# Feed-forward part of a decoder step: a loop of four passes on five engines, and the same work written out

## What is computed

```python
def residual_update(x, conv_o, pool_o, nsa_o, w_out, g2, w_gu, w_down):
    x = x + jnp.concatenate([conv_o, pool_o, nsa_o], axis=-1) @ w_out
    gu = rmsnorm(x, g2) @ w_gu
    return x + (jax.nn.silu(gu[..., :D_FF]) * gu[..., D_FF:]) @ w_down
```

## Time and profile before

| | us |
|---|---|
| median of 3 runs | 1573.87 |
| lowest and highest of them | 1573.78, 1579.42 |
| the profiled execution, its own time | 1573.92 |
| its span, first to last instruction | 1572.1 |
| from gu(2) to gu(10) in it | 574.73 |

### The profile page before, as it was taken

One profiled execution on the slowest core, in us unless ns is written; L12 is line 12 of the kernel. 1 busy time (PEld: TensorE's weight loads), 2 busy tenths in 40 slices (PEclk: granted clock), 3 DMA queues, 4 the chain that ended last, 5 costly groups with the idle time before them and its releaser, 6 DMA issues.

```text
span 1572.1 us, 22952 instructions
## 1 busy us (share of the span) xinstructions
PE 1481.1 (94%) x8743; PEld 1346.4 (86%) x8743; DVE 769.4 (49%) x1538; ACT 473.6 (30%) x950; POOL 263.8 (17%) x326
## 2 busy tenths in 40 slices
PE   6999999987999999899999999999999999999993
PEld 6999987656667666799999999999999999999992
DVE  5499942017988775322425242434344343425364
ACT  5112125035666666423212112111111111112112
POOL 2114104014322200144210101010000001010005
PEclk9999999999999999999999999999999999999996
DMA  8721206620000001233111120202020211202012
GB/s 207 187 62 29 64 8 185 192 69 1 1 1 1 1 1 41 55 83 82 54 34 48 38 71 12 71 16 69 16 67 25 60 44 39 74 11 71 17 38 111
DMA packets 148766, 88.63 MB, mean 56 GB/s; under 512 B 34466, under 2 KB 145017, under 8 KB 148577
## 3 DMA queue, kind: packets, MB, share of 16 engines
q1 hardware_dynamic: 146161, 78.22, 17.8%
q0 software_dynamic: 2496, 8.88, 2.1%
HBM read 78.33 MB, written 13.19 MB: 58 GB/s over the span
## 4 chain that ended last, share of the span: by engine, by line
PE 84%; DVE 6%; issue 3%; ACT 3%; POOL 1%; DMA 1%; SPq 1%; ACTq 0%; DVEq 0%; POOLq 0%
PE psC L1005 16%; PE psB L1005 16%; PE psA L1005 15%; PE psD L977 6%; PE psA L725 4%; PE psC L674 4%; PE psB L725 4%; PE psC L725 3%; PE psD L674 2%; PE psA L1034 2%; PE psC L1034 2%; PE psB L1034 2%; PE psA L855 1%; DVE ybuf L1559 1%; POOL accf L2096 1%
## 5 line engine op out<-in xcount | busy, mean ns | idle before, releaser
L2087 POOL TENSOR_TENSOR hid<-hid,rstdB 128x352 f32<-128x352 f32 x66 | 74.7, 1162 | 653.9 <-ACT hid L1404 653.9
L1345 ACT CAST wH<-wraw 128x1024 fp32r<-128x1024 f32 (+1 forms) x140 | 89.5, 643 | 213.4 <-PE psC L1005 93.3
L977 PE MATMUL psD<-probTb,kvtok 128*128 128x512 f32 x264 | 135.0, 594 | 3.2 <-ACT featT L1337 3.1
L1786 DVE TENSOR_TENSOR wL<-wraw,wH 128x1024 fp32r<-128x1024 f32 (+1 forms) x140 | 111.9, 800 | 42.6 <-ACT wH L1345 42.6
L1005 PE MATMUL psA<-gH,wH 128*128 128x352 f32 x352 | 114.4, 325 | 0.6 <-DVE wL L1786 0.6
L1005 PE MATMUL psB<-gH,wH 128*128 128x352 f32 x352 | 113.7, 323 | 0.0
L1005 PE MATMUL psC<-gH,wH 128*128 128x352 f32 x352 | 113.5, 323 | 0.0
L1005 PE MATMUL psA<-gH,wL 128*128 128x352 f32 x352 | 113.0, 321 | 0.0
L1005 PE MATMUL psA<-gL,wH 128*128 128x352 f32 x352 | 112.9, 321 | 0.0
L1005 PE MATMUL psC<-gL,wH 128*128 128x352 f32 x352 | 112.9, 321 | 0.0
L1005 PE MATMUL psB<-gH,wL 128*128 128x352 f32 x352 | 112.8, 321 | 0.0
(11 more groups left out here) (408 smaller groups left out, 4011.7 us busy)
## 6 DMA issues: line engine op xcount, KB each, us to landing
wraw<-in_w_gu SPq DMA_DIRECT2D x44, 512.0 KB
wraw<-in_w_down SPq DMA_DIRECT2D x88, 128.0 KB
zraw<-in_w_in SPq DMA_DIRECT2D x12, 512.0 KB
xa<-in_x_prompt SPq DMA_DIRECT2D x8, 512.0 KB, 8.3
pages<-in_cache_cmp_kv SPq DMA_DIRECT2D x32, 128.0 KB, 2.4
xs<-in_x_prompt SPq DMA_DIRECT2D x8, 512.0 KB, 3.7
out_y_prompt<-xo SPq DMA_DIRECT2D x8, 512.0 KB, 4.9
out_new_win_sample<-in_cache_win_kv POOLq DMA_DIRECT2D x1, 4064.0 KB, 22.8
```

The lines of the kernel that those rows point to most:

```text
L977: mm = pe.matmul(o, kvtok[:, kt, vc:vc + P], pt, start=first, stop=((g, br) == ORDER[-1] and x == len(g_tiles(n)) - 1))
L1345: sc_.copy(wH[:, par, 0:nk, :], wraw[:, par, 0:nk, :]).then_inc(s["wH_done"], 1)
L1786: dve.tensor_tensor(wL[:, par, 0:nk, :], wraw[:, par, 0:nk, :], wH[:, par, 0:nk, :].bitcast(F32), ALU.subtract).then_inc(s["wL_done"], 1)
L2087: pool.tensor_tensor(hid[:, n, :], hid[:, n, :], rstdB[:, c0:c0 + cw], ALU.mult).then_inc(s["up_scaled"], 1)
```

## The change

The loop is gone from `ffn_order`. A Python loop writes the nine pairs dn(f), gu(f + 2) one after the other for all five engines, with f and w as constants. The order of jobs, the work in each and all waits keep their sense. Lines move up by 1 (ahead of `ffn_order`) or 6 (behind it).

```diff
-        def ffn_order(eng, gu, dn):
+        def ffn_order(gu, dn):
             gu(0, WB)
             gu(1, WB + WGU)
-            at = WB + 2 * WGU
-            with eng.Fori(0, NLOOP) as t:
-                for x in range(2):
-                    w = t * (2 * (WGU + WDN)) + (at + (WGU + WDN) * x)
-                    dn(t * 2 + x, w)
-                    gu(t * 2 + (x + 2), w + WDN)
-            f = 2 * NLOOP
-            at += f * (WGU + WDN)
-            dn(f, at)
-            gu(f + 2, at + WDN)
-            dn(f + 1, at + WDN + WGU)
-            dn(f + 2, at + 2 * WDN + WGU)
+            w = WB + 2 * WGU
+            for f in range(NF - 2):
+                dn(f, w)
+                gu(f + 2, w + WDN)
+                w += WDN + WGU
+            dn(NF - 2, w)
+            dn(NF - 1, w + WDN)
...
-            ffn_order(sp, load_gu, load_dn)
+            ffn_order(load_gu, load_dn)
...
-            ffn_order(pe, gu, dn)
+            ffn_order(gu, dn)
```

More of the change, by code:

```diff
@@ L54 @@
 NF = KF // FT
-NLOOP = (NF - 3) // 2
 WB = KD
@@ L1419, in _ @@
             gu_par = [0]
-            ffn_order(sc_, gu, dn)
+            ffn_order(gu, dn)
             base = 3 * KD * (NF - 1) + 1
@@ L1886, in _ @@
             gu_par = [0]
-            ffn_order(dve, gu, dn)
+            ffn_order(gu, dn)
             scale_back(KD - 2)
@@ L2088, in gu @@
                                            ).then_inc(s["up_scaled"], 1)
-            ffn_order(pool, gu, lambda f, w: None)
+            ffn_order(gu, lambda f, w: None)
             pool.wait_ge(s["unit_mm"], WB + NF * WGU + (NF - 2) * WDN)
```

## The result

The changed kernel takes 1556.47 us (median of 4 runs, 1555.25 to 1557.59). The kernel before took 1574.59 beside it (4 runs, 1573.78 to 1579.42). The ratio is 0.9878, 95% interval 0.9856 to 0.9901: 1.2% faster.

The account below looks back on a forecast made before the run. PE, busy 94% of the span, was taken to bound the kernel. Three branches save 14.48 us, less 0.6 for a late load: 13.9 off 1573.92 gives 1560.0 us, range 1557.5 to 1566.0.

Parts of the forecast that it names:

- What bounds it, and where: Feed-forward part: PE busy 94% of the span, so time is saved only where PE stops, between passes.
- PE's stops at three places: At dn(2) and two later pass boundaries: removing PE's taken branches back saves 4.48, 5.52 and 4.48, together 14.48 us.
- The wait taken off, 0.76 us: PE's wait inside a pass for the weights of m = 1, absent at branches, returning three times; already subtracted from 14.48.
- The reading of the gaps: At each branch PE fetches the target's piece, gets three matmuls, waits for the next piece, then runs at a lower clock.
- Register instructions go on all five engines: Feed-forward loop: 85 register instructions a pass on PE hide beside matmuls, so removing them was costed at nothing.
- The bound of 0.9 us: Most that register instructions on ACT and DVE could cost at PE's 0.76 us wait: a tenth of a microsecond, nine places.
- One more delayed load, 0.6 us: Later gu: sliding instruction fetches delay one more w_gu load, costing 0.6 us; bounds -0.8 to 6.6 us.
- the low end: Whole kernel: lower limit of the forecast range, 1557.5 us, allowing 0.8 for no late weights and 0.9 for registers.
- Waits for weights in place of the gaps: Rival, chance 0.11: w_gu loads come late at most of the eight later gu, leaving about 1565 us.
- Gaps that stay: Rival, chance 0.05: the branch is cheap and gaps belong to starting a dn, so time stays 1573.6 to 1574 us.
- The clock: Rival, chance 0.03: PE running some 850 us without rest is granted the lower clock; 60 us of it gives 1585.

## Why PE fetched its loop anew in each pass

The body has 1813 instructions on PE. "Runtime: NRT & Kernel Launch" in the Trainium skill, section on instruction fetch mechanics, gives blocks of 16 KiB, 256 instructions each, and 2048 instructions of room for PE. By that the body fits, in 7.1 blocks. The same section of the Trainium skill also says that a taken branch whose target is not among the two current blocks stalls for a fetch; by that it would not be held. The trace of before has the stall: in 956 to 1398 us its queue fetched 30 pieces. Three kernels ask why. The first only adds a hint at the head of each pass that names the branch and its target; the second leaves out work to make the body shorter; the third has a body that can't fit.

```diff
-            with eng.Fori(0, NLOOP) as t:
+            with nc.Fori(0, NLOOP, engines=[eng.engine], hint_back_edge=True) as t:
```

> The loop of before, with a hint instruction at the head of each pass, on every engine, that names the branch and its target. Theory (the gaps are PE fetching the code that a taken branch leads to): the first gap of each place goes, since the target is fetched ahead, and the second may stay, for the next piece is asked for only then: 4 to 14 us less than before, 1560 to 1570. Rival (the gaps are the start of a dn or the branch's own handling): the hint changes nothing, 1574 within 1 us.

Measured: 1560.26 us, ratio 0.9919 (0.9897 to 0.9941). Windows of this kernel, gu(3) to gu(4) and gu(4) to gu(5), and all its DMA queues between 956 and 1398 us:

```profile
933.88:1004.01 70.13, 69.21 (x433) 68.70 (x433) 27.68 (x54) 12.56 (x24) 6.73 (x6) 1.00 0.16 45
1004.01:1074.01 70.00, 69.24 (x433) 68.72 (x433) 27.58 (x54) 12.49 (x24) 6.73 (x6) 1.00 0.15 45
```
```profile
## 3 DMA queue, kind: packets, MB, share of 16 engines
q1 hardware_dynamic: 38560, 19.14, 14.9%
issues: line engine op xcount, KB each, median us to landing
```

The row q8 is missing: not one instruction is fetched in three passes, both gaps are gone, and a branch back costs 0.13 us. The theory was too small. The hint does not bring the target earlier here: with it PE no longer loses the target.

The next kernel has no hint. It leaves out one of the three products in the gu of the loop, so 192 matmuls in a gu instead of 288, 672 in the body instead of 864.

```diff
-                    for wt, mv in ((wH, mH), (wH, mL), (wL, mH)):
+                    for wt, mv in ((wH, mH), (wH, mL), (wL, mH))[0:3 if low else 2]:
...
-                    unit(w + x, x % 2, KD, gH, gL, free)
+                    unit(w + x, x % 2, KD, gH, gL, free, low=isinstance(f, int))
```

> The loop of before, no hint, head where it was; PE leaves out the product of the weights' low part with the data in the eight gu of the loop, so its body has 672 matmuls, 1429 instructions (5.6 pieces of 16 KB) instead of 1813 (7.1), and a pair takes about 54 us. Theory (PE keeps about eight pieces; the piece behind the loop's end, fetched ahead of the branch, throws out the piece with the head, and each piece after it likewise): with room to spare nothing is thrown out: instruction fetches stop after the first pass until the last, and no issue gap over 0.3 us stands at the three places. Rival (a branch back always fetches its target, whatever the body's size): two fetches and two issue gaps of 1.3 to 2 us stay at each.

Its windows, gu(3) to gu(4) across the branch, and gu(4) to gu(5); its queues from 936 to 1288 us; and PE's waits from 865 to 1320:

```profile
918.51:973.53 55.02, 54.19 (x337) 53.68 (x337) 27.68 (x54) 12.56 (x24) 6.72 (x6) 1.00 0.20 58
973.53:1028.70 55.17, 54.29 (x337) 53.71 (x337) 27.70 (x55) 12.53 (x24) 6.72 (x6) 1.00 0.20 57
```
```profile
## 3 DMA queue, kind: packets, MB, share of 16 engines
q1 hardware_dynamic: 39104, 19.40, 19.0%
issues: line engine op xcount, KB each, median us to landing
```
```profile
PE psB L1005 <- DVE wL L1787: 6.0, 8, 0.8
PE psA L1005 <- DVE wL L1787: 0.2, 1, 0.2
```

No fetch and no issue gap, with the same loop and the same head. (Its time of 1439.67 us is that of less work.) So a body of 5.6 pieces stays on the chip and one of 7.1 does not, unless hinted. The two blocks of the Trainium skill are too few for both runs. How much PE keeps can be narrowed by counting. Thirty fetches in three passes are ten a pass. With its head ten instructions before the end of a piece, the body of before lies in nine pieces, and PE fetches the one behind it as well. With the head at the start of a piece it lies in eight, and there the queue has three transfers fewer over the span than the 79 of rows 8, so nine a pass:

```profile
q8 instruction: 76, 1.25, 0.3%
```

The body of 1429 lies in seven and, with the one behind, makes eight, which are kept. This fits the Trainium skill's 2048 instructions, eight blocks, if the piece behind the end takes the place of the oldest, which holds the head, and so on round the loop. But the hinted body lies in nine if its head is where it was, and its fetches up to 955 us come at the same points as in the kernel before. None of the nine is fetched again, and eight places do not hold nine. No record shows which piece is thrown out, so how PE keeps the hinted body stays open.

The last pair has two passes of four pairs, so one branch back and a body that is twice as long, without and with the hint (the diff is `Fori(0, 2)` with `range(4)` and factors of 4 for 2).

> Two passes of four pairs, so one taken branch back, between gu(5) and gu(6), head where it was, registers in all eight pairs. Theory (4.5 to 5.5 us a branch, 0.30 us a pair for registers): gu(5) to gu(6) 74 to 76 us, the seven others 70.0, gu(2) to gu(10) 564.5 to 565.5; some 9 us less than before, 1564 to 1565. Rival (the cost grows with the size of the body): the one place takes 10 us or more.

> As the kernel with two passes, with the hint at the head of each. The body is 3500 instructions and more, which PE can't have kept, so here the hint must bring the head's piece ahead of the branch. Theory (the hint steers the fetch): instruction fetches every 20 us all through both passes, but the place between gu(5) and gu(6) takes 70.1 to 70.5 us, or some 72.5 if only the first gap goes and the second stays, since the head lies near the end of its piece. Rival (the hint only helped because all of the body stayed on the chip): the place takes 74 to 76 us as without it.

Measured: 1564.13 us (ratio 0.9936, 0.9914 to 0.9958) and 1559.73 (0.9919, 0.9891 to 0.9946). The window from gu(5) to gu(6) of the first, then that of the second with its queue of instructions in 956 to 1398 us:

```profile
1076.06:1150.40 74.34, 71.06 (x434) 70.26 (x433) 28.55 (x54) 12.79 (x24) 5.71 (x6) 0.98 0.15 44
```
```profile
1073.43:1143.57 70.14, 69.22 (x434) 68.70 (x433) 27.67 (x54) 12.57 (x24) 6.73 (x6) 1.00 0.16 46
...
q8 instruction: 23, 0.38, 0.4%
```

One branch costs 4.3 us with a body of twice the length, so the price is one of the place, not of the size. With the hint it is 0.14 us although PE fetches all the time. So the hint does both: PE keeps this body of 1813 instructions with it, and has the target ahead of the branch where the body is too long to keep.

## Fetches and the gate weights

A fetch that starts while SP's load of gate weights runs was seen to delay gu(2) before, and in the changed kernel gu(7). The next kernel moves PE's code. It was meant to move it by 40 instructions.

```diff
             for m in range(KD):
                 out_unit(m)
+            for _ in range(20):
+                pe.matmul(bank[7][:, 0:8], ident, ident[:, 0:8], start=True, stop=True)
```

> The changed kernel, with 20 matmuls of 8 columns more on PE ahead of the feed-forward part: its code moves by 40 instructions, so PE fetches about 3.2 us earlier against the pairs. The fetch hit gu(7) when it began 7.0 us ahead, and did nothing from 12.7 to 9.8 or from 3.7 us ahead on. Theory (a fetch that starts in the load of the gate weights delays them): no wait for wL at gu(7), and waits of 0.2 to 0.6 us at gu(2) and gu(9), whose fetches move to 6.9 and 6.2 us ahead. Rival (the hit is chance from run to run): it stays at gu(7), or goes anywhere. The time within 1 us of the changed kernel, 2 us for the added matmuls aside.

PE's waits in this kernel, 865 to 1440 us, and the added matmuls in its timeline:

```profile
PE psB L999 <- DVE wL L1782: 5.4, 8, 0.7
```
```profile
743.77 5.17 PE L1036 MATMUL psD<-cpk 128*128 128x8 f32 x40
```

The wait at gu(7) went, as expected; those expected at gu(2) and gu(9) did not come. The twenty matmuls written stand in the trace as forty matmuls and forty weight loads, so the code moved by 80 instructions, and the fetches by some 6 us in place of 3.2. That ahead of gu(2) started 9.6 us before it, that ahead of gu(4) 6.75 us before it and did next to nothing (0.07 us).

The 14 profiles of this case together say more. Take the moment at which a gu would have started, its start less PE's idle time just ahead of it. A fetch 5.3 to 5.7 us ahead of that moment came with such an idle time each time, eight of eight, 0.56 to 1.09 us. One 6.6 to 6.9 us ahead did so twice in nine, with 0.25 at gu(7) of the changed kernel and 0.09 at gu(7) of the version further down. Other idle times at the start of a gu were 0.35 (fetch 2.7 us ahead), 0.12 (11.6 ahead), 0.07, and 0.16 in the kernel with the short body, where no fetch was near, so a load can be a little late without one.

Between 3.6 and 5.3 us and between 5.7 and 6.6 us ahead no profile has a fetch. So the hit depends on the moment, as was thought, and the time in which a fetch costs over half a microsecond is at most 3 us long, not the 4 to 5 us of the load. The kernels without the loop on PE had one such idle time or none in nine gu.

The kernel also took 1564.01 us (ratio 0.9943, 0.9925 to 0.9961), 7.5 more than the changed one. The added matmuls took 5.1 us in place of the 2 allowed for: they start 0.11 us apart, and 0.21 from 747.5 on, where the clock fell. Its windows, 745 to 749, then gu(0):

```profile
745.00:749.00 4.00, 4.00 (x31) 4.00 (x31) 2.09 (x2) 1.99 (x2) 1.36 (x2) 0.81 0.04 8
749.00:755.00 6.00, 6.00 (x23) 6.00 (x24) 0.00 (x0) 0.00 (x0) 0.00 (x0) 0.56 0.55 172
```

Gu(0) to gu(1) took 2.5 us more for it.

## The part ahead of gu(0), and a second profile of before

> The kernel before once more, for a second profile. Theory (the three places and 0.30 us a pair are the kernel's, the 1.5 us ahead of the feed-forward part is spread between executions): gu(2) to gu(10) 573 to 576 us with the same six issue gaps, and gu(0) starts anywhere between 743 and 750. Rival (the start of the feed-forward part moved with the change): gu(0) starts at 745.3 within 0.3 us.

Measured: 1576.12 us. Its window from gu(3) to gu(4), and PE's waits from 866 to 1440:

```profile
935.35:1009.28 73.93, 69.55 (x434) 68.69 (x433) 28.00 (x55) 13.49 (x25) 6.72 (x6) 1.00 0.15 44
```
```profile
PE psA L1005 <- issue: 10.1, 6, 2.5
PE psB L1005 <- DVE wL L1786: 3.8, 5, 0.8
PE psA L1005 <- DVE wL L1786: 2.1, 2, 1.1
```

The three places and the pairs of 70.00 are the kernel's own: gu(2) to gu(10) is 574.8 us again. That the sums agree is in part chance. Two loads of gate weights were late here, by 1.09 and 1.02 us, and with these taken off the three places cost 2.8, 4.2 and 5.7 us, 12.8 together. At the first of them PE stood for 1.30 and 2.00 us, and the clock did not fall (1.00 in the window above). The first matmul of gu(0) starts at 746.8 (745.3 in the first profile). In the other profiles, whose code up to there is the same but for the shifted one, it starts anywhere from 742.8 to 749.6, and at 743.8 in the changed kernel. So 1.50 us are within this spread. This spread is also why medians of kernels that differ by 1 us do not rank them.

## A version that beats both

The changed kernel leaves one wait in each pair, the weights of m = 1 at psB. They wait for ACT and DVE to finish the hidden values, which are needed later.

```diff
@@ ACT, gu
                     round_w(w + (x + 1), (x + 1) % 2, FT if nxt_dn else KD)
+                    if nxt_dn:
+                        round_w(w + (x + 2), (x + 2) % 2, FT)
@@ DVE, gu, x odd, behind the product of chunk y
+                        if y == 0 and nxt_dn:
+                            rest_w(w + (x + 2), (x + 2) % 2, FT)
```

`dn` leaves these two steps out at its m = 0 in turn, except in the last dn.

> The changed kernel, with the weights of m = 1 of each dn rounded by ACT ahead of its three casts of hidden values, and the low part made by DVE behind the first of its three products, instead of both last. Theory (the 0.67 us that PE waits at psB ten times are these weights, and nothing else is late there): the ten waits go, a pair takes 69.0, 6.7 us less, 1549.8. Rival (the banks are late next, since DVE frees them 0.4 us later): waits of 0.2 to 0.7 stay at psB, 0 to 4 us less.

Measured: 1549.09 us, ratio to before 0.9847 (0.9830 to 0.9863). This interval just touches that of the changed kernel (from 0.9856); the pairs of the two are clear of each other. The window from gu(3) to gu(4):

```profile
931.50:1000.28 68.78, 68.78 (x434) 68.75 (x433) 27.55 (x54) 12.72 (x24) 6.72 (x6) 1.00 0.16 47
```

PE is busy 68.78 of 68.78 us, and from gu(0) to the last dn the view of waits has no row of PE. A pair is 0.92 us shorter, not 0.70: a wait shown as 0.67 of idle costs 0.94, since the matmuls at its edges no longer overlap (starts at 979.51 and 980.51 in the changed kernel, 0.16 apart otherwise).

## Why the prediction was right and wrong

- **What bounds it, and where.** Right. PE's stops at three places were most of the loop's price, and they went as a whole. 14.48 us was the right size of this term for the two profiles compared; a second profile of the kernel before has 12.8 for it, so that it holds to 2 us and not to 0.1. The wait taken off, 0.76 us, does come back, with 0.67.
- **The reading of the gaps.** Right that they are fetches. The dear part was the second fetch right behind the first, from the head's place near the end of a piece (4.0 of 4.5 us). The prediction described it and did not price it apart.
- **"Register instructions go on all five engines. ... I cost them at nothing."** This is the step that failed. It measured 2.40 us in the eight pairs. The argument was that a pair that is half out of the loop takes 70.03, no less than one inside. But between the starts of gu(9) and gu(10) only dn(8) is out of the loop, and the start of gu(9) is in it. The two cuts also lie differently: from first matmul to first matmul (1368.08 to 1438.02) this pair takes 69.94. The wait of dn(8) at psB is no proof either, since DVE's own end of the loop stands in the chain just ahead of it. The first dn clear of the loop is dn(9), and its wait was 0.67 us already in the trace of before, 1440 to 1500 us:

```profile
PE psB L1005 <- DVE wL L1786: 0.7, 1, 0.7
```

  The bound of 0.9 us looked at this handover alone, and it holds for it (0.09 each). The other, at the start of a gu, has the rest, and the chain of waits of before had it. The first 48 matmuls of gu(9), in the loop, and of gu(10), behind it:

```profile
1368.15 7.85 PE psA L1005 x48
...
1438.18 7.64 PE psA L1005 x48
```

  That is 0.21 us for each gu in the loop, to be read beforehand. In the chain of the changed kernel the row of gu(3) is like the second:

```profile
931.17 7.64 PE psA L999 x48
```

- **One more delayed load, 0.6 us.** The disturbances of the eight pairs grew by 0.66 us, but the delay of gu(2) went, which the 0.64 from gu(0) to gu(2) are, so that the sum is nothing. The price of a hit was about right (0.6 to 0.82 taken, idle times of 0.25 to 1.09 seen). The count was not: it took the whole load as the time that hurts. The rest behind gu(10), 0.34, is within what the other profiles spread there (133.4 to 134.2).
- **Ahead of gu(0).** 1.50 us of the difference are within the spread of where gu(0) starts, and nothing ties them to the change. The range had no term for the spread between executions, though the runs shown reached from 1573.78 to 1579.42. Registers and this spread together put the time under the low end.
- **The rivals.** Waits for weights in place of the gaps: seen once in nine gu, 0.25 us. (Its range was added up wrong: a gain of 8 to 11 us gives 1563 to 1566, not 1562.5 to 1568.) Gaps that stay: no. The Trainium skill's 2048 instructions of room do not contradict this: the body of 1813 is kept with the hint and lost without it. Its rule that a taken branch out of the fetched window stalls agrees with the trace (3.43 us idle at the first place), but its window of two blocks does not, since a branch back over 5.6 of them needed no fetch. The clock: 870 us at 1.00, so it does not fall for want of a pause.

## What to carry to other kernels

A loop on the engine that bounds the kernel costs what its branch back costs there, and that is readable: compare the stretch across the branch with one inside a pass. Here writing it out was worth most because PE did not keep the body; a shorter body, a hint at the head, or a head at the start of a piece got most of it (0.1 to 0.5 us a branch in place of 4.5) without a longer program. Then look at handovers: register instructions showed no cost under a queue of work, and 0.30 us a pair where one engine hands over to another.

## What the runs showed of the hardware

- A far branch's price on PE went from 0.2 us (straight code, matmuls issued ahead) to 0.46 (head at the start of a piece) and 2.8 to 5.7 (head ten instructions before the end of one), the last with a fall of the clock to 0.5 behind it at all places but that of 2.8.
- PE ran three passes of a 1813-instruction body without a fetch when hinted, and fetched 30 pieces in the same time when not. It ran a body of 1429 without a fetch and without a hint. It fetched ten pieces a pass where the body lay in nine, and nine a pass where it lay in eight.
- Forty matmuls of 8 columns, each with its weight load, took 5.1 us, and the clock fell to 0.5 from 747.5 to 754.3 us, among them and behind them, with PE shown busy throughout.
